# A streaming encoder on one Trainium2 core: the sums of the squares of X move from VectorE to GpSimd

## The reference, cut to what matters

```
x += 0.5 * post1(SwiGLU_1(pre1(x)))
x += post2(concat(mla, mlstm, hgrn2)(pre2(x) @ W_in) @ W_out)
x += 0.5 * post3(SwiGLU_2(pre3(x)))

def rmsnorm(x, g):
    y = x * rsqrt(mean(x * x, axis=-1) + EPS)
    return y * g
```

## Time and profile before

| | |
|---|---|
| Median of 3 runs | 2688.03 us (2686.11 to 2688.68) |
| The profiled execution | 2683.46 us in all, span 2681.7 us |
| PE busy | 2598.0 us, 97% of the span |
| DVE, ACT, POOL busy | 1681.1, 1131.6 and 418.0 us |
| Mean granted clock of PE | 0.995 |

### The profile page before, as it was taken

How to read it: one execution, slowest core, us unless ns; L and a number is a source line. 1 busy time by engine, 2 the same in 40 slices (tenths; PEclk the granted TensorE clock), 3 DMA queues, 4 the chain that set the end, 5 groups by cost and what they waited for, 6 DMA issues and landing times.

```text
span 2681.7 us, 44652 instructions
## 1 busy us (share of the span) xinstructions
PE 2598.0 (97%) x17839; PEld 2479.4 (92%) x17839; DVE 1681.1 (63%) x2689; ACT 1131.6 (42%) x1901; POOL 418.0 (16%) x346
## 2 busy tenths in 40 slices
PE   8999999999899999999999999999989999999998
PEld 8999999996679999999999999989966798999998
DVE  5666574637666766657487574755576758657474
ACT  5343344415544434334354342543164435434253
POOL 0010112002134001011200110120022340011011
PEclk9999999999999999999999999999999999999999
DMA  3323223220016132232313223233101161332232
GB/s 110 91 79 91 83 69 104 71 58 11 24 43 86 52 91 79 79 94 69 87 45 95 84 69 89 84 93 82 27 10 34 38 111 37 92 95 69 73 91 74
DMA packets 370034, 191.78 MB, mean 72 GB/s; under 512 B 38525, under 2 KB 365520, under 8 KB 369870
## 3 DMA queue, kind: packets, MB, share of 16 engines
q1 hardware_dynamic: 365870, 179.08, 25.2%
q0 software_dynamic: 4000, 10.47, 1.7%
HBM read 183.58 MB, written 5.93 MB: 71 GB/s over the span
## 4 chain that ended last, share of the span: by engine, by line
PE 89%; DVE 6%; ACT 3%; issue 2%; DMA 0%; DVEq 0%; SPq 0%; ACTq 0%
PE ps L700 26%; PE ps L702 25%; PE ps L701 25%; PE ps L1034 2%; PE ps L1043 1%; PE ps L1162 1%; PE ps L1094 1%; DVE w L2064 1%; ACT w L1462 1%; PE ps L1140 1%; DVE y L2296 1%; DVE at L2501 1%; PE ps L1076 1%; DVE xl L2280 1%; PE ps L1141 1%
## 5 line engine op out<-in xcount | busy, mean ns | idle before, releaser
L700 PE MATMUL ps<-xh,w 128*128 128x320 f32 x2304 | 719.9, 312 | 18.7 <-DVE xl L2280 11.1
L702 PE MATMUL ps<-xh,w 128*128 128x320 f32 x2304 | 714.4, 310 | 0.0
L701 PE MATMUL ps<-xl,w 128*128 128x320 f32 x2304 | 714.3, 310 | 0.0
L1462 ACT ACTIVATE w<-raw 128x512 fp32r<-128x512 f32 (+3 forms) x393 | 345.5, 890 | 499.5 <-PE ps L702 478.4
L700 PEld LDWEIGHTS ps<-xh,w 128*128 128x128 f32 x2304 | 434.3, 188 | 29.8 <-DVE xl L2280 18.4
L700 PE MATMUL ps<-hh,w 128*128 128x320 f32 x1408 | 438.0, 311 | 3.3 <-DVE ub L2214 1.2
L702 PE MATMUL ps<-hh,w 128*128 128x320 f32 x1408 | 435.1, 309 | 0.0
L701 PE MATMUL ps<-hl,w 128*128 128x320 f32 x1408 | 435.0, 309 | 0.0
L701 PEld LDWEIGHTS ps<-xl,w 128*128 128x128 f32 x2304 | 434.5, 189 | 0.3
L702 PEld LDWEIGHTS ps<-xh,w 128*128 128x128 f32 x2304 | 434.7, 189 | 0.0
L2861 POOL TENSOR_TENSOR hl<-ub,hh 128x640 fp32r<-128x640 f32 x88 | 174.7, 1985 | 1499.1 <-ACT hh L1462 1401.0
(11 more groups left out here) (401 smaller groups left out, 4009.1 us busy)
## 6 DMA issues: line engine op xcount, KB each, us to landing
raw<-in_w_ffn_in_dram SPq DMA_DIRECT2D x178, 512.0 KB
raw<-in_w_ffn_out_dram SPq DMA_DIRECT2D x192, 192.0 KB
raw<-in_w_in_dram SPq DMA_DIRECT2D x38, 512.0 KB
raw<-in_w_ffn_out_dram SPq DMA_DIRECT2D x64, 128.0 KB
raw<-in_w_out_dram SPq DMA_DIRECT2D x12, 512.0 KB
out_dram<-xio SPq DMA_DIRECT2D x5, 512.0 KB
xin<-in_x_prompt_dram SPq DMA_DIRECT2D x1, 2048.0 KB, 8.5
y<-in_cache_ckv_dram POOLq DMA_DIRECT2D x8, 256.0 KB, 3.3
```

Of the source, the lines that this page charges most:

```text
L700: pe.matmul(out, wh, xh, start=first, stop=False, skip_group_check=loose)
L701: pe.matmul(out, wh, xl, start=False, stop=False, skip_group_check=loose)
L702: return pe.matmul(out, wl, xh, start=False, stop=last, skip_group_check=loose)
L1462: return nc.scalar.activation(out, in_, func, **kw)
```

## The change

The seven adds of each place leave VectorE's `lo_of_x`, and GpSimd makes them in a new function `sum_x`, with the same waits and the same semaphores. `sum_x` is called three times in a layer: ahead of each feed-forward and ahead of `mla`.

```diff
@@ -2280,11 +2280,6 @@
             V.scalar_tensor_tensor(out=XL[:, c, cut], in0=X[:, c, cut], scalar=gain(l, 16 * pre + c),
                                    in1=XH[:, c, cut].bitcast(F32), op0=ALU.mult, op1=ALU.subtract)\
                 .then_inc(xl_ready.sem, 1)
-            if cut.stop == T and c:
-                dve.wait_ge(*sq_ready.nth(l, SQ_PRE[pre] + c))
-                if c >= 2:
-                    dve.wait_ge(*pre_added.nth(l, ADD * pre + c - 2))
-                V.tensor_tensor(SX, SX, GB[:, c % 2, :], ALU.add).then_inc(pre_added.sem, 1)
 
@@ -2876,6 +2871,15 @@
                 G.tensor_tensor(SY, SY, GB[:, k % 2, :], ALU.add).then_inc(sq_added.sem, 1)
+
+        def sum_x(l, pre):
+
+            for c in range(1, KD):
+                pool.wait_ge(*sq_ready.nth(l, SQ_PRE[pre] + c))
+                if c >= 2:
+                    pool.wait_ge(*pre_added.nth(l, ADD * pre + c - 2))
+                held(pool)
+                G.tensor_tensor(SX, SX, GB[:, c % 2, :], ALU.add).then_inc(pre_added.sem, 1)
 
@@ -3033,10 +3037,13 @@
         for l in range(LAYERS):
+            sum_x(l, 0)
             ffn(l, 0, FFN0)
+            sum_x(l, 1)
             mla(l)
             recurrent(l)
             sum_y(l, 1)
+            sum_x(l, 2)
             pool.wait_ge(stored, (l + 1) * (16 * LAYER_STORES))
             ffn(l, 1, FFN1)
```

## The result

| | before | after |
|---|---|---|
| Median of 4 runs each | 2688.36 us (2686.11 to 2690.08) | 2704.62 us (2703.12 to 2705.20) |
| Ratio | | 1.006, 95% interval 1.0043 to 1.0078 |
| Profiled execution, in all and span | 2683.46, 2681.7 us | 2704.15, 2702.3 us |

The account below looks back on a forecast made before the run. PE, busy 97% of the span, was taken as the bound. Losses of 0.96, 0.45 and 0.37 us made 1.78 us a place, 8.9 us over five places, giving 2697.0 us against 2688.03, range 2689 to 2707.

Parts of the forecast that it names:

- GpSimd gets in only where VectorE has a gap: In VectorE's chunk loop: GpSimd's add enters only at the one gap per chunk, between `y` and `x`.
- (a): Before `xl` of chunk 3: adds of chunks 1 and 2 leave VectorE and return on GpSimd; PE's loss grows by 0.96 us.
- The price of a guest: On VectorE: each GpSimd add that shuts it out costs about 1.22 us, against 0.74 us for its own add.
- (b): Chunks 4, 5 and 6: VectorE needs 3.67 us a chunk against PE's 3.52, so PE waits 3 x 0.15 = 0.45 us.
- (c): Chunk 7: GpSimd takes VectorE's gap; `xl` comes 2.13 us after chunk 6, PE wants it at 1.76; costs 0.37 us.
- (d): End of a place: last add ends 1.44 us behind last `xl`, PE's sums read it 1.82 behind; 0.4 us to spare.
- (e): Weight splits behind the adds on VectorE: PE needs them at 499.5 us, giving 3 us of cover.
- (f): First place, at the kernel's start: VectorE's work comes 3.4 us later, free because PE takes the sums only at 47.7.
- No meeting that counts: Rival for the five places: GpSimd's adds hardly delay VectorE; -2.3 us, 2685.8 us, no measurable change; chance 0.18.
- The late sums: Rival at each place's end: a weight split delays the last add, PE stands 1.3 us; +6.5 us, 2703; chance 0.07.
- The dearer lock: Rival: whole 1.57 us counts, or GpSimd also enters between `x` and `xl`; 3.9 us a place, 2707; chance 0.15.
- the gap-only rule: The main forecast's rule that GpSimd enters only at VectorE's gaps; its mechanism had chance 0.60, with 6 to 13 us.

## Why the prediction was right, and where its size came from

**The mechanism** was right: GpSimd's reading sum and VectorE's instructions with two tensors in SBUF exclude each other, so the adds came back dearer than they left, and PE, only 0.33 us a chunk behind VectorE, began to wait. The memsets show that it is this and not the lag of a slower engine. That it takes two tensors in SBUF on VectorE's side stands in the trace of the kernel before, beside the sum over Y of 428.46, 1.58 us long:

```profile
428.51 0.82 DVE L2225 TENSOR_TENSOR y<-ps,y 128x640 f32<-128x640 f32 x1
429.24 1.61 DVE L2080 TENSOR_TENSOR w<-raw,w 128x768 fp32r<-128x768 f32 x1
```

The first reads one of its two tensors from PSUM (`ps`). It lies wholly under the sum and takes the 0.82 us that it takes alone (at 426.69). The second reads two from SBUF and takes 1.61 us, where it takes 0.96 at 427.63. That a locked pair of ports is the cause is what the Trainium skill says (SBUF — State Buffer, section "SBUF: two separate sides"); the trace agrees that it takes a GpSimd instruction that reads (a memset costs VectorE nothing). The section's "for the whole instruction" the runs don't bear out: VectorE waited 0.46 us of a copy that took at least 1.81 us. That it is ports at all, no run here can show.

**"GpSimd gets in only where VectorE has a gap"** is the step that failed. I drew it from 127.12. In the five places GpSimd also got in where VectorE had no gap: between the weight split and `y`, `x` and `xl`, `xl` and `y`, and `xl` and `xl`. That changes (a): not two guests but three stand ahead of `xl` of chunk 3, for the square of chunk 3 is ready in time. 3 x 1.31 less 2 x 0.74 is 2.45 us, and PE's rows give 2.5, where I had 0.96. It also made `y` and `xl` the ones that pay, not `x`.

**The price of a guest**, 1.22 us, was 1.31, since an instruction that stands right behind another would have started 0.08 before its end, not 0.03 after. So a chunk is 3.76 us, not 3.67, and (b) is 3 x 0.25 = 0.75 rather than 0.45.

**(c)** was 0.37 forecast and is 0.36: of the two `xl` of 492.71 the first, chunk 6, takes 2.21 us in a shorter window of the timeline, to 494.92, and the second ends at 497.04: 2.12 us against 1.76. The three terms give 3.6 us a place, which is what three places lost; the 0.4 us more of the two others is PE's lower clock, which no term of mine had.

**What cost nothing, as forecast.** (d) The last sum ends at 496.35, PE's sums start at 498.96: more to spare than the 0.4 us I had, since GpSimd did not come a gap late. (e) The last weight split ends at 500.51, and PE needs it where it did before, 4.6 us behind the start of its sums, at 503.6. (f) The first place: 26.28 and 26.27 us. The loads moved behind the adds start at 496.30, and the two that wait for the norm at 502.41, 0.6 us behind it; no wait for them appears.

**The rivals.** "No meeting that counts" is out by the longer rows of VectorE. The late sums are out: nothing on PE waits for GpSimd. "The dearer lock" is the one that the size leans to: 3.6 us a place, 4.1 with the lower clock, against its 3.9. Half of its mechanism was what happened (GpSimd also gets in between `x` and `xl`), and half was not (the whole 1.57 us). I gave it 0.15 and the gap-only rule 0.60; one row of one kind of clash bore the latter, and the 16 us lie between the two.

## What to carry to other kernels

Before an elementwise instruction goes from VectorE to an idle GpSimd, look in the trace for a GpSimd instruction of its kind beside VectorE ones with two inputs in SBUF: if the latter become longer there, the move costs VectorE more than the instruction did. How far VectorE runs ahead of the engine it feeds (here 0.33 us a chunk) says whether that price is paid in time. If an add is in the way of something urgent, first try to put it behind that on its own engine; here the trace showed 0.45 us a place for it, too little for the clock to tell.

## What I had not expected of the hardware

- GpSimd enters between two back-to-back VectorE instructions in the sums of X, but was passed over at 127.12 and, with 0.22 us of lead, at 126.01.
- A scaled copy of 128x640 on GpSimd takes 1.81 us or more, longer than a sum of two tensors (1.56), and yet holds VectorE up for 0.46 us where the sum does for 1.31.
- Memsets of the same tile by GpSimd, 0.63 us each, hold VectorE up by nothing, and a sum on GpSimd holds up no VectorE instruction that reads one of its two tensors from PSUM (428.51).
- PE's granted clock fell to its lower level for 3.4 us behind a wait of 1.95 us in two places (917.2, 2251.8) and not in three others with the same wait.
